# Attention in head pairs: split queries and keys, a 64-partition product, and scaling on GpSimd

## What is computed

```python
s_c = einsum('bqghd,bngd->bghqn', qg, k_cmp)          # branch 0: 63 compressed keys
p_c = masked_softmax(s_c, cmp_end <= tq)
imp = einsum('bghqn,nj->bgqj', p_c, overlap)          # which blocks of 64 keys count, per query
idx = top_k(where(valid, imp + 1000 * forced, -1e30), 8)
s_s = einsum(qg, k_s[idx])                            # branch 1: selected blocks, causal
s_w = einsum(qg, k_w[window of 512])                  # branch 2: sliding window, causal
o   = g0 * softmax(s_c) @ v_cmp + g1 * softmax(s_s) @ v_s + g2 * softmax(s_w) @ v_w
```

## Time and profile before

| | |
|---|---|
| median of 3 runs | 3602.28 us (3601.93 to 3602.37) |
| the profiled execution, first to last instruction | 3600.1 us (the median lies 2.2 us above it) |
| TensorE busy / VectorE / ScalarE / GpSimd | 3400.8 / 1516.6 / 1263.7 / 68.5 us |
| attention, windows from 536.0 to 1248.6 us | 712.6 us |
| mean granted TensorE clock | 0.974 |

### The profile page before, as it was taken

How to read it: one execution, slowest core, us unless ns; L and a number is a source line. 1 busy time by engine, 2 the same in 40 slices (tenths; PEclk the granted TensorE clock), 3 DMA queues, 4 the chain that set the end, 5 groups by cost and what they waited for, 6 DMA issues and landing times.

```text
span 3600.1 us, 42673 instructions
## 1 busy us (share of the span) xinstructions
PE 3400.8 (94%) x16738; PEld 2750.8 (76%) x16738; DVE 1516.6 (42%) x2597; ACT 1263.7 (35%) x2039; POOL 68.5 (2%) x199
## 2 busy tenths in 40 slices
PE   6999987899999999999999999999966999999998
PEld 4778876777887787788888887777854788888886
DVE  5432237766656343442342443274266332212223
ACT  4542125555555422231221223274433231313131
POOL 0000000000000010000000000010000000000000
PEclk9999998999999999999999999999977999999999
DMA  3111320000000141111111113100100211111111
GB/s 119 41 40 60 106 82 1 1 1 1 1 1 1 39 164 47 41 47 53 47 47 49 50 53 110 41 1 18 42 18 1 94 41 47 52 47 47 48 51 64
DMA packets 46249, 163.21 MB, mean 45 GB/s; under 512 B 6096, under 2 KB 7376, under 8 KB 45728
## 3 DMA queue, kind: packets, MB, share of 16 engines
q1 hardware_dynamic: 37152, 126.55, 10.8%
q0 software_dynamic: 8960, 34.77, 2.5%
HBM read 144.53 MB, written 16.78 MB: 45 GB/s over the span
## 4 chain that ended last, share of the span: by engine, by line
PE 76%; DVE 6%; ACT 2%; issue 1%; DMA 0%; POOL 0%; DVEq 0%; ACTq 0%
PE PS L223 52%; PE PS L754 6%; PE PS L727 5%; PE PS L741 3%; PE PS L1360 2%; PE PS L240 2%; PE PS L1336 2%; PE PS L1349 1%; PE PS L775 1%; PE PS L763 1%; DVE SST L1658 1%; DVE SST L1654 1%; PE PS L262 0%; PE PS L1503 0%; DVE AMT L1638 0%
## 5 line engine op out<-in xcount | busy, mean ns | idle before, releaser
L201 DVE TENSOR_TENSOR WLO<-RAW,WHI 128x1024 fp32r<-128x1024 f32 x220 | 269.4, 1225 | 1325.2 <-ACT WHI L196 1325.2
L196 ACT CAST WHI<-RAW 128x1024 fp32r<-128x1024 f32 x220 | 231.4, 1052 | 1635.6 <-PE PS L223 1604.9
L223 PE MATMUL PS<-HHI,WHI 128*128 128x512 f32 x2176 | 679.4, 393 | 5.5 <-DVE W L1112 3.6
L223 PE MATMUL PS<-HLO,WHI 128*128 128x512 f32 x2176 | 671.0, 390 | 0.0
L223 PE MATMUL PS<-HHI,WLO 128*128 128x512 f32 x2176 | 670.4, 389 | 0.0
L223 PEld LDWEIGHTS PS<-HHI,WHI 128*128 128x128 f32 x2176 | 407.5, 188 | 97.8 <-issue 9.0
L223 PEld LDWEIGHTS PS<-HHI,WLO 128*128 128x128 f32 x2176 | 408.9, 188 | 85.4
L223 PEld LDWEIGHTS PS<-HLO,WHI 128*128 128x128 f32 x2176 | 408.8, 188 | 85.4
L223 PE MATMUL PS<-HID_HI,WHI 128*128 128x512 f32 x864 | 266.7, 390 | 2.1 <-DVE HID_LO L1121 2.1
L223 PE MATMUL PS<-HID_LO,WHI 128*128 128x512 f32 x864 | 266.7, 390 | 0.0
L223 PE MATMUL PS<-HID_HI,WLO 128*128 128x512 f32 x864 | 266.4, 390 | 0.0
(11 more groups left out here) (308 smaller groups left out, 4191.5 us busy)
## 6 DMA issues: line engine op xcount, KB each, us to landing
RAW<-in_w SPq DMA_DIRECT2D x220, 512.0 KB, 3.5
X<-in_x SPq DMA_DIRECT2D x8, 512.0 KB, 6.1
merged<-W POOLq DMA_DIRECT2D x8, 512.0 KB, 3.5
gate<-W POOLq DMA_DIRECT2D x8, 512.0 KB, 5.0
W<-gate POOLq DMA_DIRECT2D x8, 512.0 KB, 3.9
W<-merged POOLq DMA_DIRECT2D x8, 512.0 KB, 4.6
X<-in_x POOLq DMA_DIRECT2D x8, 512.0 KB, 9.9
x_kept<-X POOLq DMA_DIRECT2D x8, 512.0 KB, 8.3
```

What stands on the lines that cost most here:

```text
L196: nc.scalar.copy(WHI[:, slot, :], RAW[:, slot, :]).then_inc(w_hi, 1)
L201: nc.vector.tensor_tensor(WLO[:, slot, :], RAW[:, slot, :], WHI[:, slot, :].bitcast(F32), ALU.subtract).then_inc(w_lo, 1)
L223: last = nc.tensor.matmul(o[:, half], w[:, slot, cols], x(k)[:, half], start=(k == 0 and w is WHI and x is hi), stop=(k == kcs - 1 and w i ...
```

## The change

Heads are worked on in pairs m (64 in all). Queries and keys are kept as high part and rest in float32r. In QS the high part of a segment's queries fills the group's own 64 partitions and the rest fills the other 64; in KHD[g] the high part of the keys stands in both halves. One product over 128 partitions then gives high by high plus rest by high. A second, over the group's 64 partitions only, adds high by rest of the keys (KLO). The product of the two rests is left out.

```diff
     def pe_scores(pe, n):
         s, qt, g, j = where(n)
-        q = Q[:, j, P * qt:P * qt + P]
+        pe.wait_ge(q_lo, s + 1)
+        for branch in range(2):
+            (waits for the branch's own shift two heads or one head before)
...
             for c in range(lo, hi, 512):
-                m = min(512, hi - c)
-                last = nc.tensor.matmul(ps[:, c - lo:c - lo + m], q, keys[:, c:c + m], start=True, stop=True)
+                end = min(c + 512, hi)
+                out = scores_of(n, branch)[:, c - lo:end - lo]
+                nc.tensor.matmul(out, QS[s % 2][:, j, :], KHD[g][:, branch, c:end], start=True, stop=False)
+                last = nc.tensor.matmul(out, QS[s % 2][half_of(g), j, :], KLO[half_of(g), branch, c:end],
+                                        start=False, stop=True)
```

The keys are split between the G1 units, where zeroing and copying of keys falls away; the queries of a segment one segment ahead:

```diff
+    def act_keys_hi(act, g, other):
+        nc.scalar.copy(KHD[g][half_of(1 - g if other else g), :, :], KF[half_of(g), :, :]).then_inc(k_hi, 1)
+    def dve_keys_lo(dve, g):
+        nc.vector.tensor_tensor(KLO[half_of(g), :, :], KF[half_of(g), :, :],
+                                KHD[g][half_of(g), :, :].bitcast(F32), ALU.subtract).then_inc(k_lo, 1)
+    def act_queries_hi(act, s):
+        nc.scalar.copy(QS[s % 2][rows, :, :], Q[rows, :, P * qt:P * qt + P]).then_inc(q_hi, 1)
+    def dve_queries_lo(dve, s):
+        nc.vector.tensor_tensor(QS[s % 2][half_of(1 - s % 2), :, :], Q[rows, :, P * qt:P * qt + P],
+                                QS[s % 2][rows, :, :].bitcast(F32), ALU.subtract).then_inc(q_lo, 1)
```

A chunk is now two key tiles of both heads, and the value product has 256 columns. O_PS is double. Compressed scores go through the ring of T_PS and are copied to SBUF by ScalarE:

```diff
-        return [t[i:i + 4] for i in range(0, len(t), 4)]
+        return [t[i:i + 2] for i in range(0, len(t), 2)]
...
+    def pe_use(pe, m, i):
+        for x, (branch, kt) in enumerate(chunk):
+            last = nc.tensor.matmul(O_PS[m % 2], (VS, VW)[branch][:, kt, :], PT[u % 4][:, 2 * x:2 * x + 2, :],
+                                    start=False, stop=(u + 1 == used_at[m + 1] and x == len(chunk) - 1))
...
+    def act_cmp_scores(act, s):
+        nc.scalar.copy(EC[:, :, :], T_PS[c % 2].rearrange("p (h n) -> p h n", n=HEAD)).then_inc(pt_copied, 1)
```

The scaling goes to GpSimd, the reciprocal stays on VectorE:

```diff
-            nc.vector.tensor_scalar(p[:, 0:w], p[:, 0:w], HINV[:, n % 2, branch:branch + 1],
-                                    GATE[:, qt, col:col + 1], ALU.mult, ALU.mult).then_inc(p_done, 1)
+    def pool_probs(pool):
+        for n in range(HEADS_ALL):
+            pool.wait_ge(inv_done, n + 1)
+            for branch in range(2):
+                nc.gpsimd.tensor_scalar(p, p, HINV[:, n % 8, branch:branch + 1], GATE[:, qt, col:col + 1],
+                                        ALU.mult, ALU.mult).then_inc(p_done, 1)
```

The order on TensorE and ScalarE (`ahead` is two pairs on in tiles 0 to 3, one pair on from tile 4):

```diff
+        for m in range(PAIRS_ALL):                      # pe_attention
+            pe_scores(2 * ahead)
+            (first pair of a segment: pe_cmp_scores(s + 1); third pair: pe_cmp_turn(s + 1))
+            pe_turn(m, 0); pe_turn(m, 1); pe_cmp_values(m); pe_use(m, 0)
+            pe_scores(2 * ahead + 1)                    # for m = 31 only after the last pe_use
+            for i in range(1, chunks): pe_turn(m, i + 1); pe_use(m, i)
+        for m in range(PAIRS_ALL):                      # act_attention
+            (first pair of a segment: act_cmp_scores(s + 1), act_queries_hi(s + 1); third: act_cmp_copy(s + 1))
+            for i in range(chunks):
+                act_copy(m, i); (i = 0: act_out_hi(m - 1))
+                the exponentials of the pair ahead, two after i = 1, one each after i = 2 and 3
```

More of the change, by code:

```diff
@@ L599, in act_compress @@
     def act_compress(act, t):
[L600 to L603, removed]
+        if t in (3, 4):
+            for g in range(N_GROUPS):
+                act_keys_hi(act, g, t == 4)
+        if t == 5:
+            act_queries_hi(act, 0)
         if t == 3:
@@ L687, in where, with heads_of @@
     def where(n):
-        s = n // HPG
-        return s, s // 2, s % 2, n % HPG
+        s, pair, e = n // HPG, n % HPG // 2, n % 2
+        return s, s // 2, s % 2, 4 * (pair % 2) + 2 * e + pair // 2
+    def heads_of(m):
+        first = where(2 * m)[3]
+        return slice(first, first + 3, 2)
     N_SHORT = 4 * 2 * HPG
+    PAIRS_SHORT = N_SHORT // 2
     short = lambda n: n < N_SHORT
-    PSEL_S = [sb(f"PSEL_S{i}", [512], X_AT + 8 * KB + 2 * KB * i) for i in range(3)]
-    PWIN_S = [sb(f"PWIN_S{i}", [512], X_AT + (16, 18, 29)[i] * KB) for i in range(3)]
@@ new lines, in scores_of, with width_of, ahead_of, waits_for_all @@
+        return PS[:, at_n:at_n + 512] if short(n) else PS[:, at_n:at_n + (5 * P if branch else T)]
+    def width_of(n, branch):
+        return P * min(where(n)[1] + 1, 5 if branch else QT)
+    def ahead_of(m):
+        if m + 2 < PAIRS_SHORT:
+            return m + 2
+        return m + 1 if PAIRS_SHORT <= m + 1 < PAIRS_ALL else None
+    def waits_for_all(m):
+        return m + 1 == PAIRS_SHORT
+    def exp_after(m, chunks):
+        return [chunks - 1] * 4 if waits_for_all(m) else [min(i, chunks - 1) for i in (1, 1, 2, 3)]
@@ L744, in pe_values @@
-    def pe_values(pe, n):
-        s, qt, g, j = where(n)
-        chunks = chunks_of(qt)
-        v = (VS, VW)
-        def use(i):
-            pe.wait_ge(pt_copied, turned_at[n] + i + 1)
-            u = used_at[n] + i
-            for x, (branch, kt) in enumerate(chunks[i]):
-                last = nc.tensor.matmul(O_PS, v[branch][:, kt, :], PT[u % 4][:, x, :], start=False,
-                                        stop=(i == len(chunks) - 1 and x == len(chunks[i]) - 1))
-            last.then_inc(pv_done, 1)
-        if not short(n):
-            pe_turn(pe, n, 0)
-        pe.wait_ge(pt_copied, c_turned_at[s] + 1)
-        if n:
-            pe.wait_ge(o_free, n)
-        nc.tensor.matmul(O_PS, VCZ[j % 2][:, :], PCT[s % 2][:, j // 2, :], start=True, stop=False)
-        for i in range(1, len(chunks)):
-            if not short(n):
-                pe_turn(pe, n, i)
-            use(i - 1)
-        use(len(chunks) - 1)
+        pe.wait_ge(q_lo, s + 1)
@@ new lines, in pe_turn @@
+    def pe_turn(pe, m, i):
+        qt = qt_of(m)
+        c = turned_at[m] + i
+        if c >= 2:
+            pe.wait_ge(pt_copied, c - 1)
+        for x, (branch, kt) in enumerate(chunks_of(qt)[i]):
+            first = max(0, qt - 4) if branch else 0
+            if kt == first:
+                pe.wait_ge(p_done, 4 * m + 3 + branch)
+            for e in range(2):
+                src = probs_of(2 * m + e, branch)[:, P * (kt - first):P * (kt - first) + P]
+                last = nc.tensor.transpose(T_PS[c % 2][:, P * (2 * x + e):P * (2 * x + e) + P], src, IDENT[:, :])
+        last.then_inc(t_done, 1)
@@ L977, in dve_attention @@
+        dve_inverse(dve, 3)
+        for m in range(PAIRS_ALL):
+            s, pair, ahead = m // PAIRS, m % PAIRS, ahead_of(m)
+            if ahead:
+                dve_shift(dve, 2 * ahead, 0)
+                dve_shift(dve, 2 * ahead, 1)
             if s + 1 < SEGS:
-                if j == 1:
+                if pair == 0:
+                    dve_queries_lo(dve, s + 1)
                     dve_cmp_shift(dve, s + 1)
-                if j == 2:
+                if pair == 1:
                     dve_cmp_probs(dve, s + 1)
-                if j == 3:
@@ L1843, in _ @@
             pool.wait_ge(s_, 16 * g1_tiles(i))
+        pool_probs(pool)
         pool_merge(pool)
```

318 lines of the change are left out of this document (160 added, 158 removed).

## The result

The kernel after takes 3627.09 us (median of 4 runs, 3623.74 to 3629.93), the kernel before on the same chip 3602.11 (4 runs, 3600.34 to 3602.37): ratio 1.0068, 95% interval 1.0054 to 1.0083. It is slower by 25 us, where 9 us less were forecast: within the wide range (3525 to 3640), outside the forecast's own (3570 to 3612), and in the other direction. The profiled execution spans 3628.1 us, 28.0 more than that of before.

The account below looks back on a forecast made before the run. TensorE, busy 94%, was taken as the bound, with VectorE in tile 0. Segments (701.4 us) plus 2 made 703.4 against 712.6, so -9 us: span 3591, median 3593, own range 3570 to 3612, wide range 3525 to 3640.

Parts of the forecast that it names:

- the price of a change: TensorE's scores: each change of row count costs 0.20 us in or out, 0.14 with 128 columns; 132 us in all.
- the short stage: Attention's query tiles 0 to 3: 239.6 us forecast, where the kernel before took 262.5.
- the long stage: Attention's query tiles 4 to 7, TensorE busy throughout: 461.8 us forecast, where the kernel before took 450.1.
- the waits of the short stage: Waits added per segment in query tiles 1 to 3: 2 us in tile 1, 1.5 in tiles 2 and 3.
- rival B: ScalarE's exponentials wait for VectorE, delaying copies for TensorE: 1.0 us a long-stage pair, 0.5 short; 3633 us, chance 0.21.
- the 35: Query tiles 0 to 3 together: 239.6 us forecast, 274.6 measured, 35.0 over the forecast sum.
- 22 us, now above TensorE's 17.1: Tile 0, per segment: VectorE's loop and selection chain take 22 us, more than TensorE's 17.1; before it was 25.8.
- A: Rival, TensorE's scores: changing row count is cheap for fp32r; 3534 us if only idle counts, 3461 if nothing; chance 0.20.
- C: Rival, GpSimd's scalings in the attention come late, from 3.3 ns a column on: 3633 us, chance 0.09.
- the two bounds: GpSimd's scaling price: as fast as VectorE (0.61 us for 640 columns), or fully proportional at 4.05 ns a column.
- D: Rival, TensorE's scores: small fp32r products run at the fp32 rate; 3615 us, chance 0.08.

Follow-up runs that it names:

- the rests together: Kernel after with all 128-partition products of a head first and its 64-partition products after them: 3538.39 us, ratio 0.9822.
- Full rows: Kernel after with the product with the rests of the keys over all 128 partitions instead of 64: 3510.47 us, ratio 0.9746.
- The late selection: Kernel after with only the selection and its mask moved behind the second head's shifts and reciprocals in the short stage: 3611.58 us, ratio 1.0024.
- all 128 rows: Kernel after with the selection and mask moved later and the key-rest product over all 128 partitions: 3489.08 us, ratio 0.9681.
- together_late: Kernel after with each head's 64-partition products after its 128-partition ones, and selection and mask moved later in the short stage: 3517.79 us, ratio 0.9763.

## Why the prediction was wrong

**Right: the price of a change.** It came from one place with small transposes and held for 512-column products to the hundredth, and in tile 6 with the rests together (17.1 for 17.0). Full rows removed 117 us where 132 were booked. The two agree less than they seem to: 51 us less of low clock are in the 117, up to 26 us by the half-length estimate, and against that TensorE's idle time in the attention grew by 30 us, most of it in the short stage, where other engines hold it once it has less to do. What the Trainium skill says in "TensorEngine Tiling (Array Packing)", Key Properties, that a change of the mode drains the array, agrees with these rows; the price is the rows'.

**Partly luck: the long stage.** 461.8 forecast, 463.3 measured, but tiles 4 to 6 took 109.0, 114.3, 121.6 us where 105.4, 112.6, 119.6 were forecast, and tile 7 118.3 where 124.2 was. Two terms were missed and cancel. Scores are made ahead, and the windows hold 244 of the 256 products over 128 partitions that the forecast booked there: those of three heads, some 8 us, lie in the row of tile 3 (tile 7 has 52 of 64). And the clock was low for 17.1 us, some 8.5 us by the half-length estimate, where the forecast had it at full.

**Wrong, first: the waits of the short stage.** "I add 2 us of waits in tile 1, 1.5 in tiles 2 and 3", for each segment. I had summed what each engine does and not gone through the order in which ScalarE meets VectorE's long chain. It is rival B's mechanism, and I looked for it in the wrong stage: priced at 1.0 us a pair in the long stage, where there is none, and 0.5 in the short, 16 us for its 32 pairs. The late selection shows 14.0 us of the 35 to be this (11.1 in tile 1, 4.1 in tile 3, 0.3 in tile 2, and 1.5 given back in tile 0). Most of it isn't the waits themselves but the low clock that came with them: 23.9 us of it in tiles 1 to 3, and 1.7 with the late selection.

**Wrong, second: the clock.** "22 us, now above TensorE's 17.1" took tile 0 at full clock, with 0.82 before my eyes. At 1.2 GHz TensorE's own work is the bound: the first segment of the late selection is 32.0 us at 0.50. Tile 0 is 13.3 us over its forecast in the kernel after and 14.8 with the late selection; with all 128 rows it is 46.6, 2.6 over. That the changes decide is shown. How much of the 12.2 us between 58.8 and 46.6 is the clock can only be estimated: in together_late tile 0 takes 46.6 us too, at 64 rows, with half as many changes. Those were booked at 4.5 us, and 27 us less of low clock are worth up to 13.5, while TensorE's idle time grows by 3.6. So the clock is the larger part. What brings it down and keeps it down stays open. What remains of the 35, some 6 us in tiles 1 to 3 with the late selection, holds about 2 us of scores made ahead for later heads; the rest was not looked into.

**The rivals.** A (the change cheap) is wrong, by the spacings and by full rows. B is right in kind, as said, but its long-stage term is nothing. It doesn't explain the direction alone: with the late selection the kernel is still 0.24% slower than before. C (GpSimd late) is wrong: 0.88 us for 640 columns, and GpSimd itself waits for reciprocals. That lies near the lower of the two bounds (0.61 and 2.59 for 640 columns). From 451 ns for 128 columns and 1198 for 1024 it is 0.83 ns a column and 0.34 us besides. The estimate of 1.5 ns a column from the Trainium skill's "GPSIMD Engine Reference", Performance versus the Vector engine, comes near at 640 (0.96 against 0.88), but not at 128 (0.19 against 0.45) nor at 1024 (1.54 against 1.20). The section gives that figure as the best case of an unrolled loop; for the shortest loop bodies it has 1.03 cycles an element, an estimate of 0.86 ns a column, and the measured slope agrees with this one. The fixed part isn't in it, and the measurement decides. D (128 columns at the fp32 rate) is wrong: with 128 rows in both, the two products of such a chunk take 0.17 us together, where the fp32 rate would be 0.213 for each.

## What to carry to other kernels

Two matmuls of different row counts in turn cost TensorE 0.20 us a change, nearly another 512-column pass: sum the changes before the passes, group products of one form, or give the smaller one all rows. When engines work through lists in a fixed order, follow the one long chain of an engine through every list that waits for it, stage by stage; a wait of 2 us may cost several times that if the clock falls with it (here 4 us less of waits came with 15.5 less of time). And cost a stage at the clock its row shows, not at the full one.

## What the runs showed of the hardware that was not expected

- From a pause of 2.27 us on TensorE had 13.7 us at half clock. But the clock also fell where TensorE was recorded busy all through, in the long stage of the kernel after (at 811.9, 866.5, 921.2 and 1156.7 us, for 3.4 to 6.8 us each, with no idle time at all in the 8 us before):

```profile
803.90:811.90 8.00, 8.00 (x33) 5.05 (x32) 5.48 (x15) 4.17 (x9) 2.65 (x4) 1.00 0.00 0
811.90:815.30 3.40, 3.40 (x18) 3.18 (x18) 0.00 (x0) 1.63 (x2) 0.81 (x1) 0.50 0.00 0
```

- With 128 rows in both products, and with full float32 products in their place, no such fall is in the long stage. In tile 0 the low time with 128 rows and the late selection is 17.1 and 10.2 us, with 64 rows 54.6.
- Before the first scores, 30 products that nobody needs changed nothing that can be told (3611.6 and 3613.2 us; 3489.1 and 3486.5).
- GpSimd's product with two scalars takes 0.88 us for 640 columns, VectorE's 0.61; a copy of 64 columns had taken 0.26.
- A float32r product of 128 columns starts 0.06 us before the next one when both have 128 rows, less than the 0.109 that I had taken as the floor.
